# Hybrid decoder trunk on one core: the last projection chunk in three rounded parts, and the output weights' splits moved into the recurrence's levels

## What is computed

```python
h = rms_norm(x, mix_norm[l])
p = h @ w_comb                       # (256, 1024) @ (1024, 3200 or 3216)
# columns: r, k, v (3 x 384), decay/iclr/gate inputs (128),
#          short convolution (3 x 256), attention q, k, v (3 x 384)
y = concat([rwkv7_mix(...), short_conv_mix(...), dilated_attention_mix(...)])
x = x + y @ w_o[l]
x = x + ffn(rms_norm(x, ffn_norm[l]))
```

## Time and profile before

| | |
|---|---|
| median of 3 runs | 1580.93 us (1580.54 to 1581.57) |
| the profiled execution's own time | 1580.65 us |
| its span, first to last instruction | 1578.8 us |
| TensorE busy | 1555.1 us, 98% of the span |
| VectorE busy | 1264.2 us, 80% |
| ScalarE busy | 1073.8 us, 68% |
| GpSimd busy | 80.2 us, 5% |
| mean granted TensorE clock | 0.996 of full |

### The profile page before, as it was taken

How to read it: one execution, slowest core, us unless ns; L and a number is a source line. 1 busy time by engine, 2 the same in 40 slices (tenths; PEclk the granted TensorE clock), 3 DMA queues, 4 the chain that set the end, 5 groups by cost and what they waited for, 6 DMA issues and landing times.

```text
span 1578.8 us, 28727 instructions
## 1 busy us (share of the span) xinstructions
PE 1555.1 (98%) x10958; PEld 1359.9 (86%) x10958; DVE 1264.2 (80%) x1440; ACT 1073.8 (68%) x1323; POOL 80.2 (5%) x82
## 2 busy tenths in 40 slices
PE   8999999999999998999999999999999999999997
PEld 8988999999999887888888888888888888888886
DVE  5686754444567866999999999999999999999996
ACT  5545444444446455788888888888888888888885
POOL 0022000000000400000000000000000000000000
PEclk9999999999999999999999999999999999999999
DMA  8700655555344008999999999999999999999994
GB/s 313 234 2 3 220 186 184 186 187 187 122 163 152 3 17 307 359 377 361 391 393 361 389 393 362 394 390 358 393 389 359 393 390 359 392 391 358 390 379 158
DMA packets 189944, 447.76 MB, mean 284 GB/s; under 512 B 8208, under 2 KB 10784, under 8 KB 189728
## 3 DMA queue, kind: packets, MB, share of 16 engines
q1 hardware_dynamic: 186480, 434.46, 75.5%
q0 software_dynamic: 2688, 9.44, 2.7%
q10 hardware_dynamic: 688, 2.62, 0.5%
HBM read 438.63 MB, written 6.29 MB: 282 GB/s over the span
## 4 chain that ended last, share of the span: by engine, by line
PE 96%; DVE 2%; ACT 1%; issue 1%; DMA 0%; POOL 0%; SPq 0%; DVEq 0%; ACTq 0%; POOLq 0%
PE bank L789 28%; PE bank L791 27%; PE bank L790 27%; PE bank L770 9%; PE bank L1465 2%; ACT w_hi L1544 0%; DMA ring<-in_w_in 0%; PE bank L960 0%; PE bank L810 0%; DVE w_lo L2239 0%; PE bank L1428 0%; PE bank L1214 0%; DVE w_lo L1986 0%; PE bank L1105 0%; POOL out L740 0%
## 5 line engine op out<-in xcount | busy, mean ns | idle before, releaser
L1544 ACT ACTIVATE w_hi<-ring 128x1024 fp32r<-128x1024 f32 x812 | 858.6, 1061 | 334.5 <-PE bank L791 324.5
L2239 DVE TENSOR_TENSOR w_lo<-ring,w_hi 128x1024 fp32r<-128x1024 f32 x672 | 814.4, 1224 | 62.6 <-ACT w_hi L1544 12.9
L789 PE MATMUL bank<-w_hi,acts_hi 128*128 128x512 f32 (+1 forms) x1376 | 539.7, 392 | 3.5 <-DVE w_lo L2239 3.4
L791 PE MATMUL bank<-w_hi,acts_lo 128*128 128x512 f32 (+1 forms) x1376 | 533.6, 388 | 0.0
L790 PE MATMUL bank<-w_lo,acts_hi 128*128 128x512 f32 (+1 forms) x1376 | 532.8, 387 | 0.0
L789 PEld LDWEIGHTS bank<-w_hi,acts_hi 128*128 128x128 f32 x1376 | 258.9, 188 | 55.4 <-DVE w_lo L2239 4.5
L791 PEld LDWEIGHTS bank<-w_hi,acts_lo 128*128 128x128 f32 x1376 | 258.7, 188 | 53.8
L790 PEld LDWEIGHTS bank<-w_lo,acts_hi 128*128 128x128 f32 x1376 | 259.1, 188 | 50.8
L789 PE MATMUL bank<-acts_hi,w_hi 128*128 128x256 f32 x884 | 252.4, 286 | 2.7 <-DVE acts_lo L2146 1.7
L790 PE MATMUL bank<-acts_lo,w_hi 128*128 128x256 f32 x884 | 250.1, 283 | 0.0
L791 PE MATMUL bank<-acts_hi,w_lo 128*128 128x256 f32 x884 | 250.1, 283 | 0.0
(11 more groups left out here) (247 smaller groups left out, 1112.6 us busy)
## 6 DMA issues: line engine op xcount, KB each, us to landing
ring<-in_moe_wg SPq DMA_DIRECT2D x112, 1024.0 KB, 7.1
ring<-in_moe_wu SPq DMA_DIRECT2D x112, 1024.0 KB, 7.5
ring<-in_moe_wd SPq DMA_DIRECT2D x112, 1024.0 KB, 7.1
ring<-in_w_in SPq DMA_DIRECT2D x24, 1024.0 KB, 7.8
ring<-in_dense_wg SPq DMA_DIRECT2D x14, 1024.0 KB, 5.2
ring<-in_dense_wu SPq DMA_DIRECT2D x14, 1024.0 KB, 5.1
ring<-in_dense_wd SPq DMA_DIRECT2D x14, 1024.0 KB, 4.9
ring<-in_w_o SPq DMA_DIRECT2D x8, 1024.0 KB, 7.7
```

The lines of the kernel that those rows point to most:

```text
L789: pe.matmul(out_, a_hi, b_hi, start=first, stop=False, **kw)
L791: return pe.matmul(out_, a_lo, b_hi, start=False, stop=final, **kw)
L1544: return act.activation(o, i, ACT.Copy, **kw)
L2239: TT(w_lo[:, q, :], raw, w_hi[:, q, :].bitcast(F32), ALU.subtract).then_inc(lo_ready, 1)
```

## The change

Chunk 3 joins `SPLIT_IN` and `TOGETHER`: it is multiplied in three rounded parts, with its four units side by side, piece by piece. ScalarE writes its high parts between the copies of units 6 and 7. Its low parts are written by GpSimd, which counts them in a new semaphore `pool_low`, and TensorE waits on that for each piece. `head_spread` and the bonus sums with the first scores become hooks behind the second and the third piece. The four units are copied out of PSUM in two pairs once all pieces are done, and the recurrence on TensorE waits for the first pair. GpSimd now sets up the inverse after its four low parts instead of after the last unit. The pieces 0 to 3 of `w_o` are split within the recurrence's levels 1 to 4, one in each, on ScalarE and VectorE; before, ScalarE split all four, and VectorE the first two, during chunk 3, and VectorE the other two in levels 1 and 2. Layer 0's copy of v moves from ahead of the head factors' use into level 1.

```diff
--- before.py
+++ after.py
@@ -493,12 +494,11 @@
             return got
 
 
-        SPLIT_IN = (4, 5, 2, 0, 1)
-        TOGETHER = (4, 5, 2, 0)
+        SPLIT_IN = (4, 5, 2, 0, 1, 3)
+        TOGETHER = (4, 5, 2, 0, 3)
         UNIT_BANKS = {4: (0, 0, 1, 1), 5: (2, 2, 3, 3), 6: (0, 1, 0), 2: (2, 2, 3, 3), 0: (0, 0, 1, 1), 1: (2, 3, 0, 1),
-                      3: (2, 3, 1, 0)}
-        SINGLE = (10, 11)
-        SINGLE0 = (0, 10)
+                      3: (1, 1, 0, 0)}
+        SINGLE0 = (0, 6)
         IN0 = {(l, ch): l * 4 * (len(SPLIT_IN) + 2 + 3 * NJ) + 4 * i
                for l in range(L) for i, ch in enumerate(SPLIT_IN)}
         WO0 = [l * 4 * (len(SPLIT_IN) + 2 + 3 * NJ) + 4 * len(SPLIT_IN) for l in range(L)]
@@ -536,7 +536,9 @@
         for l in range(L):
             us = units(l)
             for place, ch in enumerate(CHUNKS):
-                if ch in SPLIT_IN:
+                if ch == 3:
+                    stream += [("in", l, ch, hf, (pool_low, PIECES * l + 2 * hf + 2)) for hf in range(2)]
+                elif ch in SPLIT_IN:
                     stream += [("in", l, ch, hf, (lo_ready, IN0[l, ch] + 2 * hf + 2)) for hf in range(2)]
                 else:
                     seen = SINGLE0[l] + max(i for i, u in enumerate(singles(l)) if u[0] == place) + 1
@@ -704,7 +706,12 @@
             for l in range(L):
 
                 add_swapped(l)
-                pool.wait_ge(unit_done, SINGLE0[l] + SINGLE[l])
+                for q in range(PIECES):
+                    n = halves[("in", l, 3, q // 2)]
+                    pool.wait_ge(hi_ready, IN0[l, 3] + q + 1)
+                    pool.tensor_tensor(w_lo[:, q, :], ring[:, slot_of[n], q % 2 * PIECE:(q % 2 + 1) * PIECE],
+                                       w_hi[:, q, :].bitcast(F32), ALU.subtract).then_inc(pool_low, 1)
+                pool.wait_ge(pool_low, PIECES * (l + 1))
                 pool.tensor_copy(by_six(inv), spread(eye, 2 * HEADS)).then_inc(inv_init, 1)
                 pool.tensor_copy(by_six(invT), spread(eye, 2 * HEADS)).then_inc(inv_init, 1)
                 pool.wait_ge(b_kept, 2 * l + 2)
@@ -843,7 +850,7 @@
                     final = last_of_group(n, t, len(tiles))
                     ins = mm(bank[b][r0:r0 + SEL_STEP, 0:T], selin[:, t, :], tiles[t], first, final)
                     if t == 0 and n % 2:
-                        ins.then_inc(pc_free, PIECES)
+                        ins.then_inc(pc_free, 1)
                     if final:
                         ins.then_inc(hs_sum, 1)
 
@@ -882,6 +889,8 @@
                         ws = slice(k % 2 * CW + n % 4 * P, k % 2 * CW + (n % 4 + 1) * P)
                         last = three(b[:, 0:T], w_hi[:, k // 2, ws], w_lo[:, k // 2, ws], h_hi[:, k, :], h_lo[:, k, :],
                                      k == 0, k == KT - 1)
+                        if final and k in (1, 3, 5):
+                            last.then_inc(pc_free, 1)
                     elif kind == "cm":
                         c0 = n % 4 * P
                         last = mm(b[:, 0:T], w[:, c0:c0 + P], hT[:, k, :], k == 0, k == KT - 1)
@@ -893,7 +902,10 @@
             def project_together(l, ch, mine, us0, hooks):
 
                 for q in range(PIECES):
-                    pe.wait_ge(lo_ready, IN0[l, ch] + q + 1)
+                    if ch == 3:
+                        pe.wait_ge(pool_low, PIECES * l + q + 1)
+                    else:
+                        pe.wait_ge(lo_ready, IN0[l, ch] + q + 1)
                     if q == 0:
                         seen = max(bank_place(l, us0 + i)[2] for i in range(len(mine)))
                         if seen:
@@ -1001,7 +1013,7 @@
                 pe.wait_ge(hs_used, 2 * l + 2)
                 pe.wait_ge(rw_ready, l + 1)
                 pe.wait_ge(bonus_ready, l + 1)
-                pe.wait_ge(unit_kept, kept(l, "cm", 14))
+                pe.wait_ge(unit_kept, kept(l, "cm", 13))
                 for (h, c), (h2, c2) in zip(pairs_of((0,)), pairs_of((1,))):
                     with_a_and_r(bT, 4, h, c)
                     last = narrow(bT, aT, 1, h2, c2)
@@ -1272,7 +1284,16 @@
                         pe.wait_ge(vres_shifted, l)
                         lora_products(l, (("v", (6, 7)),))
 
-                HOOKS = {2: {1: lambda: head_spread(2 * l, 6, (5, 6, 7))}, 0: {1: lora_wa, 2: lora_g, 3: lora_v}}
+                def sum_bonus():
+                    pe.wait_ge(bonus_in, l + 1)
+                    for i in range(NRT):
+                        last = mm(bank[(4, 7)[i // 2]][:, i % 2 * T:i % 2 * T + T], const("pair"), tmp2[:, i, :])
+                    last.then_inc(bonus_sum, 1)
+                    pe.wait_ge(unit_kept, kept(l, "cm", 4))
+                    scores(l, 0)
+
+                HOOKS = {2: {1: lambda: head_spread(2 * l, 6, (5, 6, 7))}, 0: {1: lora_wa, 2: lora_g, 3: lora_v},
+                         3: {1: lambda: head_spread(2 * l + 1, 3, (5, 6)), 2: sum_bonus}}
                 for u, unit in enumerate(us):
                     ch = CHUNKS[unit[0]]
                     at = unit[1:3]
@@ -1289,16 +1310,6 @@
                         pe.wait_ge(lora_kept, LORA0[l] + LORAS[l])
                         pe.wait_ge(hs_sq, l + 1)
                         head_sum(2 * l + 1, [tmp1[:, i, :] for i in range(NRT)], 4)
-                    if at == ("cm", 13):
-                        head_spread(2 * l + 1, 3, (5, 6))
-                    if at == ("cm", 14):
-
-                        pe.wait_ge(bonus_in, l + 1)
-                        for i in range(NRT):
-                            last = mm(bank[(4, 7)[i // 2]][:, i % 2 * T:i % 2 * T + T], const("pair"), tmp2[:, i, :])
-                        last.then_inc(bonus_sum, 1)
-                        pe.wait_ge(unit_kept, kept(l, "cm", 12))
-                        scores(l, 0)
                 recurrence(l)
 
                 out_tile(l, 5, range(KT)).then_inc(pc_free, 1)
@@ -1692,6 +1703,8 @@
                             keep_tok(4 + u, tok_a[:, u * RW:(u + 1) * RW], 6 + u)
                     if lev >= 3:
                         output_squares(l, lev - 3)
+                    if lev < 5:
+                        split_out(l, lev - 1)
                 keep_probs(l, 4)
                 for u in range(2):
                     act.wait_ge(lv_done, 2 * l + u + 1)
@@ -1829,7 +1842,7 @@
                 if l:
                     keep_lora(l, 3, bonus, (6, 7), ACT.Sigmoid, "vres_v0")
 
-                for kind, n in [("cm", n) for n in (4, 5, 6, 7, 12, 13, 14, 15)]:
+                for kind, n in [("cm", n) for n in (4, 5, 6, 7)]:
                     keep_unit(l, kind, n)
                     if (kind, n) == ("cm", 5):
 
@@ -1837,11 +1850,12 @@
                         then(act.activation(inv_w.rearrange("p i (c t) -> p i c t", c=NC), w65[:, :, :, 1:C + 1],
                                             ACT.Exp, scale=DECAY))
                         act.activation(w65, w65, ACT.Exp, scale=-DECAY).then_inc(w_ready, 1)
-                    if (kind, n) == ("cm", 12):
-                        root(2 * l + 1)
-                        act.activation(root_of, eps, ACT.Exp)
-                    if n in (7, 12, 13, 14):
-                        split_out(l, (7, 12, 13, 14).index(n))
+                    if n >= 6:
+                        split_in(l, 3, range(2 * (n - 6), 2 * (n - 5)))
+                root(2 * l + 1)
+                act.activation(root_of, eps, ACT.Exp)
+                for n in (12, 14):
+                    keep_pair(l, 3, "cm", n)
                 recurrence(l)
 
                 if l:
@@ -1991,8 +2005,10 @@
                 k = WO_ORDER[i]
                 n = halves[("o", l, k // 2, 0)]
                 dve.wait_ge(hi_ready, WO0[l] + i + 1)
+                if i == 0:
+                    dve.wait_ge(pool_low, PIECES * (l + 1))
                 TT(w_lo[:, i % 4, :], ring[:, slot_of[n], k % 2 * PIECE:(k % 2 + 1) * PIECE],
-                   w_hi[:, i % 4, :].bitcast(F32), ALU.subtract).then_inc(lo_ready, 1)
+                   w_hi[:, i % 4, :].bitcast(F32), ALU.subtract).then_inc(lo_ready, 1 if i else 1 + PIECES)
 
             def h_low_part(n, k):
                 dve.wait_ge(h_high, KT * n + k + 1)
@@ -2089,8 +2105,10 @@
                         dve.wait_ge(tt_done, 10 * l + 2 * (lev - 1) + e + 1)
                         dve.wait_ge(invt_ready, 12 * l + 2 * (lev - 1) + e + 1)
                         copied(half(invT, e), lmask[:, 1, lev, :], 4 + e).then_inc(invt_ready, 1)
-                    if lev <= 2:
-                        split_out(l, lev + 1)
+                    if lev < 5:
+                        split_out(l, lev - 1)
+                    if lev == 1 and l == 0:
+                        TS(v_first, pT[:, 6:9, :], 1.0, None, ALU.mult)
                 largest_score(l, 5)
                 keep_output(l, 4)
 
@@ -2321,9 +2339,7 @@
 
                 dve.wait_ge(unit_kept, kept(l, "cm", 7))
                 then(shift(l, vT, lambda i: param(l, "mu", 6 + i), tmp1))
```

(6 more changed lines are left out.)

1 line of the change is left out of this document (added).

## The result

The changed kernel takes 1612.05 us (median of five runs, 1609.54 to 1614.51) against 1581.04 for the kernel before in the same session: the ratio is 1.0193, with a 95% interval of 1.0182 to 1.0204. It is 31.0 us slower; 22.4 were forecast, and 1609 was the top of the range. Of all executions in this document one, of the changed kernel with mended levels, took 1729.4 us at a lower granted clock (0.843) and stays out of its ratio.

What follows compares the result with a forecast made beforehand. TensorE was taken as the bound, tied with VectorE ahead of layer 1's recurrence. Late starts 8.7 + 8.0, clock 2.6 and levels 3.1 made 22.4 us on 1580.93: 1603 us, own range 1600 to 1606, whole range 1588 to 1609.

Steps and rivals of the forecast that it cites:

- Late low parts and the exclusion: Chunk 3: GpSimd's low parts hold up VectorE's reciprocal; recurrence 8.7 us late in layer 0, 8.0 in layer 1.
- the setup copies: GpSimd's two copies for the inverse may delay VectorE up to 1.7 us a layer; counted as nothing, kept for the range.
- The first rival: Chunk 3: GpSimd enters only at VectorE's pauses; three low parts precede the reciprocal, 7.65 us late; 1598 us, chance 0.34.
- The clock: Behind TensorE's 9 us waits in the projection: lower granted clock costs 1.3 us a layer, 2.6 in all.
- The levels: Recurrence levels 1 to 4: ScalarE's high parts 2.0 us in all, VectorE's later work 0.55 a layer, together 3.1.
- ScalarE's exceeded cover: Levels 3 and 4: a high part of 1.06 us exceeds 0.58 of cover; TensorE waits about 0.5 us each.
- Layer 0's copy of v stands there too: Recurrence level 1, VectorE: the copy counted within 0.55 us a layer, itself between nothing and 1.06.
- my own rule: GpSimd and VectorE exclude each other for a whole instruction; whoever waits gets in when one ends.
- the late start: Start of the recurrence behind the late reciprocal: 8.7 us later in layer 0, 8.0 in layer 1.

Runs made afterwards that it cites:

- mended levels: Changed kernel with layer 0's copy of v at its old place and the levels' `w_o` splits moved toward idle engine time: 1604.1 us, ratio 1.0141.
- the filled idle time: Changed kernel with 18 unused products put on TensorE ahead of the spread of head 1: 1606.64 us, ratio 1.0165.
- the run with v put back: Kernel before plus the `w_o` splits in the levels, with layer 0's copy of v at its old place: 1586.14 us, ratio 1.0029.
- the run with the levels alone: Kernel before plus only the `w_o` splits and the copy of v in the levels, chunk 3 unchanged: 1589.17 us, ratio 1.0045.
- the spread last: Changed kernel with head 1's spread and the bonus sum behind the fourth piece: 1608.65 us, ratio 1.0181.
- the run with two subtractions: Kernel before plus two unread GpSimd subtractions of the low parts' size in each layer: 1591.28 us, ratio 1.0059.

## Why the forecast was right in its mechanism and wrong in its size

**Late low parts and the exclusion: right.** Forecast: all four low parts ahead of the eleven vector instructions' end, the reciprocal at 98.2, a wait of some 9 us, the recurrence 8.7 us late in layer 0 and 8.0 in layer 1 at full clock. Measured: 98.03, 9.13 and 8.75, and 8.4 and 7.65. That GpSimd is the cause is shown twice, by the same delay from subtractions that nobody reads, and by its absence when VectorE writes the low parts. That the reciprocal's place came out within 0.2 us is partly luck. I had counted four GpSimd instructions at full length, 10.2 us, and the setup copies as nothing; there were six, 11.6 us, each less about 0.3 for the vector instruction that it lets in, 9.8 in all. The first rival, in which VectorE gets in more often, did not come: three scalings took three whole low parts. By these durations VectorE got one instruction between two of GpSimd, as its neighbour rows had shown.

**The clock: the term that was mis-sized.** "I add 1.3 a layer, 2.6; it could be nothing or double." It was 3.2 (spread 0.94, third piece 2.30) in layer 0 and 3.1 in layer 1 (10.74 late in all, 7.65 without the clock), and 3.2 by the filled idle time. Those two alone are 6.3. I had read the price off one fall, behind the wait of 3.26 us in the expert part, and took it for a fixed price that occurs once a layer at one place. The reading was about right (1.5 us by TensorE's products there), but the price is not fixed, and it occurs at more places where TensorE comes to stand: in the profiled execution also in level 5 of layer 0 (48 products in 2.83 us instead of 1.61), in level 5 of layer 1, and in the expert part behind the very wait that was there before, now 3.28 us:

```profile
660.00:665.00 5.00, 5.00 (x15) 0.50 0.69 227
```

Before, the clock there was 0.75 for 4 us; from that place to the end the changed kernel loses another 1.7 us. Over the runs a fall in the projection cost 1.7 us (behind waits of 1.80, 2.05 and 2.23), 2.8 (5.89) and 3.1 to 3.2 (2.47, 5.64, 8.75 and 9.13), and behind the waits for `bT` 4.1 (3.35) and 2.1 (6.13): no single fall would have given the term.

**The levels: 3.1 forecast, 7.1 measured alone and 8.0 in the kernel after.** ScalarE's exceeded cover came as said, 0.34 instead of 0.5 us. The step that failed in this term is the copy of v: "Layer 0's copy of v stands there too" was priced inside 0.55 a layer, at its old 0.56 us. I had not applied my own rule to it: it stands beside GpSimd's convolution and takes 1.63 us. With the late high part that is the wait of 1.55 us in level 2. Put back, it gives 2.5 us; the splits alone still cost 4.6. The rest is clock again: in the run with the idle time filled, layer 0's levels take 3.15 us more than before at a granted clock of 1.00 (164.11 - 108.62 = 55.49 against 152.38 - 100.04 = 52.34), in the kernel after 6.2 (170.47 - 111.93). At full clock the levels thus cost 3.15 and, by layer 1 of the run with v put back, 1.6: 4.75 against 3.1, and the difference is the wait that the copy of v makes.

**The books**, for the profiled execution (+33.8): late start 8.4 + 7.65; half clock behind the spread 3.2 + 3.1; levels of layer 0, 6.2, of layer 1, 3.3; the expert part 1.7; 0.3 in which `head_sum` came later already. The sum is 33.9. Sorted by the forecast's terms: the late start 16.1 (16.7 forecast), the levels at full clock 4.75 (3.1), and the half clock 3.2 + 3.1 behind the spread, 3.05 and 1.65 in the levels and 1.7 in the expert part, 12.7 in place of 2.6. So the step that failed is the clock term, with 10 of the 11.4 us by which this execution passes the forecast. The median execution is 2.8 us below it, and only this one has a profile.

What stays open: behind which waits the clock falls. Around the spread and the start of the recurrence it fell behind every wait of 1.8 us and more. Behind the wait of 1.55 us in level 2 it fell in the run with the levels alone and in that with the spread last, but not with the low parts on VectorE, and in the kernel after the 96 products there kept their 2.31 us and it fell in level 5, behind 0.47; and with products in the spread's wait the same waits in layer 0 left it at 1.00. No run here separates what came before such a wait from the wait itself. Open too is what sets the price of a fall: in the run with two subtractions it was 3.2 us in layer 0 and 1.7 in layer 1, behind nearly the same wait.

## What to carry to other kernels

Before work goes to an idle GpSimd, read what VectorE does in the same stretch: in every run here each GpSimd instruction on SBUF, a plain copy too, took its whole length out of a VectorE row of SBUF instructions, less one of VectorE's own. If that row is on the path, GpSimd's time is added to it, although GpSimd was idle. A stall of TensorE is priced as the wait plus the half clock behind it, here 1.5 to 4.1 us, in no order with the length of the wait, at every place where the change makes it stand, and as a range, not as one number. Splits moved into the levels cost nothing where their engine stood idle and 4.6 us half a level away, 7.1 with the copy of v: look up each engine's gaps first, and place them there.

## What the hardware did that I had not expected

A GpSimd copy of 128x1024 from SBUF to SBUF (1.09 us each in a row of four) shut VectorE out as the subtraction did (2.05 us each, and 2.42 with a rounded result). The exclusion also covers VectorE's `TENSOR_SCALAR` with one tensor source: 0.29 us each alone, three in 4.36 to 7.29 us beside GpSimd. The two engines took turns by whole instructions, so three short ones behind one another cost VectorE three of GpSimd's long ones (7.29 us beside three low parts of 2.42). And the half clock's price did not follow the idle time ahead of it: 3.2 us behind 2.47 and behind 9.13, 1.7 behind 2.23, 2.8 behind 5.89. The same wait of 3.3 us in the expert part cost 1.5 before and some 3 after.
